# Modulation weights of a two-layer decoder step: from a split pair of products to unsplit float32 in four column strips, in their own buffers

## The chip, the cores and the metric

The kernel runs on one core of a Trainium2 chip. The metric is the device time of one execution in microseconds. Three runs of the kernel before gave 3008.25, 3013.66 and 3019.26 us; their median, 3013.66 us, is the time before.

## What is computed

One inference step of a two-layer decoder for 512 prompt tokens and 8 sample tokens with a model width of 1024. Every sub-layer (feed-forward, mixing, feed-forward) is normalized and then shifted, scaled and gated by vectors that come from a condition `c` (one row for the prompt, eight for the samples, so nine rows):

```
mod = jax.nn.silu(c) @ mod_w + mod_b            # [9 rows] x [1024, 9216], per layer
sh0, sc0, gt0, sh1, sc1, gt1, sh2, sc2, gt2 = jnp.split(mod[:, None, :], 9, axis=-1)
h = modulate(rmsnorm(x, norm_pre[0]), sh0, sc0)
x = x + 0.5 * gt0 * rmsnorm(swiglu(h, ffn1_in, ffn1_out), norm_post[0])
... mixing with sh1, sc1, gt1 ...
h = modulate(rmsnorm(x, norm_pre[2]), sh2, sc2)
x = x + 0.5 * gt2 * rmsnorm(swiglu(h, ffn2_in, ffn2_out), norm_post[2])
```

`swiglu(h, w_in, w_out)` is `(silu(g) * u) @ w_out` with `g, u` the halves of `h @ w_in`; the hidden width is 2816, that is 22 tiles of 128.

## The kernel before

All large products keep float32 accuracy by splitting. A block of weights (a **chunk**: 128 partitions by 1024 float32, 512 KB) is loaded by SP into one of four slots of `stage`. ACT rounds it into `w_hi` (`split`, L856), DVE writes the remainder `lo_apart` (L1970), and TensorE multiplies high with high, high with low and low with high parts of the activations. The four slots form one ring for all weights of the program: `load` (L686) issues a chunk as soon as the chunk four before it has been split (`lo_done`), and ACT and DVE take the chunks in the same order.

A **trip** of the feed-forward input loop (`ffn_in`) makes two hidden tiles. On TensorE (L1442) these are four tiles of 48 matmuls of 260 columns: gate and up of the first hidden tile, gate and up of the second. ACT applies silu to the gate tile (`sil`, L949), DVE multiplies it with the up tile (`hidf`, L2127), ACT and DVE write its high and low part. The weights of a trip are four chunks, c0 to c3.

The modulation weights are 18 **groups** of 512 columns per layer, 36 in all, each group being 4 chunks, so 144 chunks. They go through the same ring. In the opening of layer 0, MOD_FIRST = 8 groups (32 chunks of 1024 columns) are computed before anything else. The other 28 groups run one per trip beside the feed-forward loops (`per` = 8: the four chunks of the trip alternate with four modulation chunks), in phases f1j0, f1i1, f2j0 and f2i1 of layer 0 (five trips each) and f1j0 and f1i1 of layer 1 (five and three). A modulation chunk is four matmuls of 512 columns with the silu of `c` as the stationary operand `c_st` (high and low part, 18 of 128 columns in use), done by `mod_rows` (L1313) after each of the four tiles of a trip. When the group is complete ACT copies its 18 rows (`modrow`, L960), TensorE turns them (`turn_rows`, L1322), and DVE adds the bias into `modT`.

The order within a trip is written by hand on every engine and locked by counting semaphores. What matters here:

- TensorE: the fourth tile of a trip (up of the second hidden tile) is written to the same PSUM pair 0 as the first tile of the next trip, which therefore waits for `hidf` of the second hidden tile (`pe.wait_ge(ev_d, i * 2 + ed)` in `body`, L1460).
- ACT (L941), for each of the two hidden tiles m: two splits, silu, two more splits, the high part `hid_hi`. DVE (L2113) follows with its remainders and `hidf`.
- `mod_rows` of the last chunk stands after the fourth tile, and the rows are turned after the first tile of the next trip.

```
for m in range(2):
    at = per // 2 * m
    if m or split_here(phase, i):
        split(chunk(phase, at + 2, i, per))
    split(chunk(phase, at + 3, i, per))
    ...
    nc.scalar.activation(sil[:, m, :]..., PS[:, 2 * m, :, 0:HALF], ACT.Silu)
```

## Time and profile before

| | |
|---|---|
| runs (us) | 3008.25, 3013.66, 3019.26 |
| span of the profiled execution | 3023.3 us |
| TensorE busy | 96% of the span |
| VectorE / ScalarE / GpSimd busy | 56% / 39% / 12% |
| mean DMA | 107 GB/s |

The profiled execution has no separate time beside its span; the span lies 9.6 us (0.3%) above the median of the three runs. In the profile, PE is the matmul side of TensorE, PEld its weight loads, DVE is VectorE, ACT is ScalarE, POOL is GpSimd, SP is the engine that issues the weight loads. A float32 matmul shows as two records, a matmul of rounded (fp32r) operands as one. The page's rows on the 40 slices show PE at nine tenths or more from slice 2 to 39 and the DMA queues at a quarter to a half of their capacity except in the first slice.

### The profile page before, as it was taken

The numbers are of one execution on the slowest core, as the hardware profiler recorded it, in microseconds if no ns is written. First come the engines' busy times: TensorE is split into PE (matmuls) and PEld (weight loads), VectorE is DVE, ScalarE is ACT, GpSimd is POOL, SyncE is SP. The second block draws the span as 40 slices with busy tenths as digits, with TensorE's granted clock in tenths as the row PEclk, the third lists the DMA queues.
The fourth block names the chain that finished last, engine by engine and source line by source line (L and its number), as shares of the span: only waits on it lengthen the run. The fifth ranks groups of instructions, "written<-read, shape, count | busy, mean of one in ns | idle before, by whom it ended". The sixth has DMA issues, their size and how long they took to land.

```text
span 3023.3 us, 55792 instructions
## 1 busy us (share of the span) xinstructions
PE 2908.2 (96%) x22056; PEld 2703.3 (89%) x22056; DVE 1687.8 (56%) x3427; ACT 1193.3 (39%) x2023; POOL 366.7 (12%) x426
## 2 busy tenths in 40 slices
PE   6999999999999999999999999999999999999998
PEld 5899999899776689999999999999987767999997
DVE  5443346888869475424474424378878775632234
ACT  6533333545444244323334323245453532522222
POOL 2100000324025100000010000011330431100000
PEclk8999999999999999999999999999999999999998
DMA  7443443412224334434434434232222243232321
GB/s 265 127 153 98 141 147 91 137 50 64 57 75 124 107 98 124 145 101 153 124 93 133 141 100 149 86 109 99 57 64 62 62 133 119 85 97 82 100 76 64
DMA packets 448405, 324.28 MB, mean 107 GB/s; under 512 B 25114, under 2 KB 403346, under 8 KB 447451
## 3 DMA queue, kind: packets, MB, share of 16 engines
q1 hardware_dynamic: 442810, 296.60, 32.6%
q0 software_dynamic: 5408, 25.17, 2.5%
q8 instruction: 121, 1.98, 0.3%
q14 instruction: 66, 0.53, 0.1%
HBM read 310.48 MB, written 11.24 MB: 106 GB/s over the span
## 4 chain that ended last, share of the span: by engine, by line
PE 77%; DVE 15%; issue 3%; ACT 2%; DMA 1%; POOL 0%; another core or an unknown queue 0%; ACTq 0%; SPq 0%; DVEq 0%; POOLq 0%
PE PS L1306 77%; DVE score L2514 1%; DVE lo_over L1975 1%; DVE best L2513 1%; DMA stage<-in_mod_w 1%; DVE W L2444 1%; PE PS L1538 1%; DVE score L2504 1%; DVE xT L2071 1%; DMA stage<-in_w_branch_attn 1%; DVE counting L2251 0%; DVE sm L2197 0%; DVE tmpn L2069 0%; DVE lg L2680 0%; DVE dgr L2690 0%
## 5 line engine op out<-in xcount | busy, mean ns | idle before, releaser
L1306 PE MATMUL PS<-h_hi,w_hi 128*128 128x260 f32 (+1 forms) x4000 | 830.4, 289 | 10.5 <-POOL h_lo L2897 5.8
L1306 PE MATMUL PS<-h_lo,w_hi 128*128 128x260 f32 (+1 forms) x4000 | 808.0, 284 | 0.0
L1975 DVE TENSOR_TENSOR lo_apart<-stage,w_hi 128x1024 fp32r<-128x1024 f32 (+2 forms) x448 | 492.9, 1134 | 466.4 <-ACT w_hi L863 462.5
L1306 PEld LDWEIGHTS PS<-h_hi,w_hi 128*128 128x128 f32 (+1 forms) x4000 | 623.4, 189 | 60.5 <-issue 40.3
L1306 PEld LDWEIGHTS PS<-h_lo,w_hi 128*128 128x128 f32 (+1 forms) x4000 | 618.9, 189 | 0.0
L1306 PE MATMUL PS<-h_hi,lo_apart 128*128 128x260 f32 x2816 | 567.2, 283 | 0.0
L863 ACT ACTIVATE w_hi<-stage 128x1024 fp32r<-128x1024 f32 (+3 forms) x586 | 540.9, 954 | 46.8 <-DMA stage<-in_mod_w 15.3
L1306 PEld LDWEIGHTS PS<-h_hi,lo_apart 128*128 128x128 f32 x2816 | 434.6, 189 | 0.0
L1306 PE MATMUL PS<-hid_lo,w_hi 128*128 128x260 f32 x1408 | 283.8, 283 | 0.0
L1306 PE MATMUL PS<-hid_hi,w_hi 128*128 128x260 f32 x1408 | 283.2, 282 | 0.0
L1306 PE MATMUL PS<-hid_hi,lo_apart 128*128 128x260 f32 x1408 | 282.9, 282 | 0.0
L2127 DVE TENSOR_TENSOR hidf<-sil,PS 128x520 f32<-128x520 f32 x88 | 61.3, 697 | 366.5 <-PE PS L1306 366.5
L1306 PE MATMUL PS<-h_hi,lo_over 128*128 128x260 f32 (+1 forms) x1184 | 241.1, 286 | 0.0
L955 ACT ACTIVATE hid_hi<-hidf 128x520 fp32r<-128x520 f32 (+1 forms) x88 | 56.3, 639 | 450.9 <-DVE hidf L2127 450.9
L2878 POOL TENSOR_TENSOR hs<-yT,r_s 128x64 f32<-128x64 f32 x6 | 1.9, 320 | 1853.5 <-ACT r_s L929 1853.5
L1306 PEld LDWEIGHTS PS<-hid_hi,lo_apart 128*128 128x128 f32 x1408 | 217.0, 188 | 0.0
L1306 PEld LDWEIGHTS PS<-hid_hi,w_hi 128*128 128x128 f32 x1408 | 216.8, 188 | 0.1
L1306 PEld LDWEIGHTS PS<-hid_lo,w_hi 128*128 128x128 f32 x1408 | 216.7, 188 | 0.0
L1306 PEld LDWEIGHTS PS<-h_hi,lo_over 128*128 128x128 f32 (+1 forms) x1184 | 184.8, 190 | 0.0
L1975 DVE TENSOR_TENSOR lo_over<-stage,w_hi 128x1024 fp32r<-128x1024 f32 (+1 forms) x138 | 147.2, 1069 | 23.6 <-ACT w_hi L863 22.0
L949 ACT ACTIVATE sil<-PS 128x520 f32<-128x520 f32 x88 | 53.2, 604 | 263.2 <-PE PS L1306 263.2
L1306 PE MATMUL PS<-w_hi,c_st 128*128 128x512 f32 x288 | 116.5, 424 | 11.8 <-DVE lo_apart L1975 11.4
(436 smaller groups left out, 4088.6 us busy)
## 6 DMA issues: line engine op xcount, KB each, us to landing
stage<-in_ffn_in SPq DMA_DIRECT2D x176, 512.0 KB
stage<-in_mod_w SPq DMA_DIRECT2D x144, 512.0 KB
stage<-in_w_in SPq DMA_DIRECT2D x72, 512.0 KB
stage<-in_ffn_out SPq DMA_DIRECT2D x64, 384.0 KB
stage<-in_ffn_out SPq DMA_DIRECT2D x64, 320.0 KB
stage<-in_w_out SPq DMA_DIRECT2D x16, 512.0 KB
x_hold<-xT SPq DMA_DIRECT2D x2, 2080.0 KB
xT<-x_hold SPq DMA_DIRECT2D x2, 2080.0 KB, 8.1
```

What stands on the lines that cost most here:

```text
L863: nc.scalar.activation(w_hi[:, ch.slot, 0:ch.elems], stage[:, ch.slot, 0:ch.elems], ACT.Copy)\
L949: nc.scalar.activation(sil[:, m, :].rearrange("p (a n) -> p a n", a=2), PS[:, 2 * m, :, 0:HALF], ACT.Silu).then_inc(ev_a, 1)
L955: nc.scalar.activation(hid_hi[:, bass.ds(i * 2 + (s.first_tile + m), 1), :], hidf[:, m:m + 1, :], ACT.Copy)\
L1306: return nc.tensor.matmul(out, lhsT, rhs, start=start, stop=stop)
L1538: return nc.tensor.transpose(out, in_, ident[p0:p0 + size, p0:p0 + size])
L1975: nc.vector.tensor_tensor(lows(ch)[:, ch.slot, 0:ch.elems], stage[:, ch.slot, 0:ch.elems], w_hi[:, ch.slot, 0:ch.elems].bitcast(FP32), ALU ...
L2071: nc.vector.tensor_tensor(xT[:, k, 0:T], xT[:, k, 0:T], tmpn[:, k % 2, 0:T], ALU.add).then_inc(x_ready, 1)
L2127: nc.vector.tensor_tensor(hidf[:, m, :].rearrange("p (a n) -> p a n", a=2), sil[:, m, :].rearrange("p (a n) -> p a n", a=2), PS[:, up, :, ...
L2444: own(nc.vector.tensor_tensor_scan(W4[:, r, q, 1:NCH + 1], V(6)[:, g:g + 1].to_broadcast([P, NCH]), W4[:, r, q, 1:NCH + 1], 0.0, ALU.mult, ...
L2504: i = nc.vector.scalar_tensor_tensor(sc, rl[:, n % 2, 0:(t + 1) * P], wT[:, t, h:h + 1], sc, ALU.mult, ALU.add)
L2513: own.step(nc.vector.max(best[:], sc))
L2514: own.step(nc.vector.match_replace(sc, best[:], sc, TAKEN))
```

## The change

1. The modulation products are no longer split. The weights stay float32 and are multiplied in float32 with `c32` (the nine rows of silu(c), padded to 32 columns). Four matmuls of 256 columns go to four strips of 32 PSUM partitions: in the opening the four quarters of a chunk's 1024 columns, beside the feed-forward two k-blocks by two halves of 512 columns, the k-blocks being summed when the rows are turned (`halves_sel`).
2. The modulation chunks leave the ring. In the opening they use eight slots of `mod_open`; beside the loops they use four slots of their own, `mod_stage`, with the semaphores `mod_full` and `mod_used`. The feed-forward chunks keep the ring, now with nothing between them.
3. Four groups in the opening (16 chunks), fourteen beside the first feed-forward of layer 0: two per trip in f1j0 (`rate` = 2, ten groups), one per trip in four trips of f1i1, none in its fifth (`f1j1`).
4. All four chunks of a group are multiplied together, after the tile that ends a hidden tile (both with two groups per trip, the second with one), instead of one chunk after each tile. ACT and DVE in a trip: two splits, silu, `hidf`, `hid_hi`, and nothing in between.

```
 class Chunk:
-    def __init__(self, base, shift, elems, in_place=False):
+    def __init__(self, base, shift, elems, before, in_place=False):
...
-    MOD_FIRST = GROUPS - (FT // 2 - 1)
+    MOD_FIRST = 4
...
         if l == 0:
-            ffn1 = ([Gates('f1i0', 1, 0), Gates('f1j0', n0 - 1, 2, MOD_FIRST, 0, 0, 'after plain')],
-                    [Gates('f1i1', n1, 0, MOD_FIRST + n0 - 1, 0, n0 - 1)])
+            early = 2 * (n0 - 1)
+            left = FIRST_BESIDE - early
+            ffn1 = ([Gates('f1i0', 1, 0), Gates('f1j0', n0 - 1, 2, MOD_FIRST, 0, 0, 'after plain', rate=2)],
+                    [Gates('f1i1', left, 0, MOD_FIRST + early, 0, early),
+                     Gates('f1j1', n1 - left, 2 * left, opening='after mods')])
...
 SP, the opening
-                    for g in range(MOD_PAIRS):
-                        for k in range(4 if g == 0 else 0, KD):
-                            load(chunk('mod', k, g, 8), mod_weights(g, k).unsqueeze(1))
+                    for n in range(4, KD * MOD_PAIRS):
+                        if n >= OPEN:
+                            sp.wait_ge(mod_used, n - OPEN + 1)
+                        sp.dma_start(mod_open[:, n % OPEN, :], mod_weights(n // KD, n % KD)).then_inc(open_full[n % OPEN], 16)
+
+                def mod_load(s, i, m, j):
+
+                    sp.wait_ge(mod_used, i * (4 * s.rate) + (OPENED + 4 * (s.mods_before + m) + j - 3))
+                    sp.dma_start(mod_stage[j][:].rearrange("p (k n) -> p k n", k=2),
+                                 rows_of('mod_w', 2 * j, 2, i * (512 * s.rate) + (s.group + m) * 512, 512, bass.ds(s.of_layer, 1)))\
+                        .then_inc(mod_full[j], 16)
...
 SP, a trip
                         for j in range(4):
-                            load(chunk(phase, j * per // 4, i, per),
+                            load(chunk(phase, j, i, 4),
                                  rows_of(name, 0, KD, (j % 2) * DFF + (f0 + s.first_tile + i * 2 + j // 2) * P, P))
-                            if per == 8:
-                                load(chunk(phase, 2 * j + 1, i, per),
-                                     rows_of('mod_w', 2 * j, 2, i * 512 + s.group * 512, 512, bass.ds(s.of_layer, 1)))
+                            if s.group is not None:
+                                if type(i) is int and i == j == 0 and phase in ('f1j0', 'f2j0'):
+                                    sp.wait_ge(h_lo_ready, (N + (1 if phase == 'f1j0' else 3)) * KD)
+                                if s.rate == 1:
+                                    mod_load(s, i, 0, j)
+                                else:
+                                    mod_load(s, i, j // 2, 2 * (j % 2))
+                                    mod_load(s, i, j // 2, 2 * (j % 2) + 1)
...
 ACT, a trip
                         for m in range(2):
-                            at = per // 2 * m
                             if m or split_here(phase, i):
-                                split(chunk(phase, at + 2, i, per))
-                            split(chunk(phase, at + 3, i, per))
+                                split(chunk(phase, 2 * m + 2, i, 4))
+                            split(chunk(phase, 2 * m + 3, i, 4))
...
                             nc.scalar.activation(sil[:, m, :].rearrange("p (a n) -> p a n", a=2),
                                                  PS[:, 2 * m, :, 0:HALF], ACT.Silu).then_inc(ev_a, 1)
-                            if per == 8:
-                                split(chunk(phase, at + 4, i, per))
-                                split(chunk(phase, at + 5, i, per))
...
 TensorE, products and turning
-                def mod_rows(pair, ch, j):
-
-                    pe.wait_ge(lo_done, ch.number(1))
-                    for k in range(2):
-                        for w in (w_hi, lows(ch)):
-                            last = mm(PS[:, pair, 0, :], c_st[:, 2 * j + k, :], w[:, ch.slot, k * 512:(k + 1) * 512],
-                                      start=(j == 0 and k == 0 and w is w_hi), stop=(j == 3 and k == 1 and w is not w_hi))
-                    last.then_inc(chunk_used, 1)
+                def mod_rows(s, i, m, j):
+
+                    pe.wait_ge(mod_full[j], i * (16 * s.rate) + 16 * (OPENED // OPEN + s.mods_before + m + 1))
+                    for q in range(4):
+                        odd, half = q // 2, q % 2
+                        last = mm(PS[32 * q:32 * q + 32, 3, 0, 0:256], c32[:, 2 * j + odd, :],
+                                  mod_stage[j][:, odd * 512 + half * 256:odd * 512 + half * 256 + 256],
+                                  start=(j == 0), stop=(j == 3))
+                    last.then_inc(mod_used, 1)
 
                 def turn_rows(pair):
-                    for q in range(4):
-                        last = mm(PS[:, pair, 1, q * NC:(q + 1) * NC], modrow[:, q * P:(q + 1) * P], sel18[:])
+                    by_block = PS[:, pair, 1, 0:4 * NC].rearrange("p (h q c) -> p q h c", h=2, q=2)
+                    for q in range(2):
+                        last = mm(by_block[:, q], modrow[:, q * P:(q + 1) * P], halves_sel[:].rearrange("p (h c) -> p h c", c=NC))
...
 TensorE, a trip
-                                if per == 8:
-                                    mod_rows(3, chunk(phase, 4 * m + 2 * gu + 1, i, per), 2 * m + gu)
+                                if gu == 0 and beside and (m and s.rate == 2 or not m and not (type(i) is int and i == 0)):
+                                    turn_beside(i, m)
+                                if gu == 1 and beside and (m or s.rate == 2):
+                                    for j in range(4):
+                                        mod_rows(s, i, m if s.rate == 2 else 0, j)
```

How the instructions move, at the three places of which the prediction speaks. First the queue of SP, in the loop of phase f1i1 of layer 0 (one group per trip). Before:

```order
L693 ISA [waits lo_done]
L693 DMA stage<-in_ffn_in 128x8x128
L691 REGISTER_ALU
L693 ISA [waits lo_done]
L693 DMA stage<-in_mod_w 128x2x512
L691 REGISTER_ALU
L693 ISA [waits lo_done]
L693 DMA stage<-in_ffn_in 128x8x128
```

And now:

```order
L717 ISA [waits lo_done]
L717 DMA stage<-in_ffn_in 128x8x128
L729 REGISTER_ALU
L730 ISA [waits mod_used]
L730 DMA mod_stage_84<-in_mod_w 128x2x512
L713 REGISTER_ALU
L717 ISA [waits lo_done]
L717 DMA stage<-in_ffn_in 128x8x128
```

The second feed-forward chunk of a trip (c1) stands in both behind the first modulation load; that load now waits for `mod_used`, which TensorE raises, where it waited for `lo_done`, which DVE raises.

Second, ACT in the second half (m = 1) of a trip of the same loop. Before, where the slots 2 and 3 hold c3 and the last modulation chunk of the trip itself:

```order
L862 REGISTER_ALU [waits stage_full2]
L863 ACTIVATE w_hi<-stage 128x1024 [waits chunk_used]
L862 REGISTER_ALU [waits stage_full3]
L863 ACTIVATE w_hi<-stage 128x1024 [waits chunk_used]
L947 REGISTER_ALU
L948 REGISTER_ALU [waits chunk_used]
L949 ACTIVATE sil<-PS 128x520 [waits ev_d]
```

And now, where the slots 0 and 1 hold c0 and c1 of the next trip:

```order
L902 ACTIVATE w_hi<-stage 128x1024 [waits chunk_used,stage_full0]
L899 REGISTER_ALU [waits stage_full1]
L902 ACTIVATE w_hi<-stage 128x1024 [waits chunk_used]
L983 REGISTER_ALU
L984 REGISTER_ALU [waits chunk_used]
L985 ACTIVATE sil<-PS 128x520 [waits ev_d]
```

The silu that closes a trip now stands behind the split of c1 of the next trip; before it stood behind chunks of its own trip only.

Third, TensorE at the end of a hidden tile in f1j0, now:

```order
L1340 MATMUL PS<-mod_stage_84,c 32x256 [waits mod_full0]
L1340 MATMUL PS<-mod_stage_84,c 32x256 x3
L1340 MATMUL PS<-mod_stage_85,c 32x256 [waits mod_full1]
L1340 MATMUL PS<-mod_stage_85,c 32x256 x3
L1340 MATMUL PS<-mod_stage_86,c 32x256 [waits mod_full2]
L1340 MATMUL PS<-mod_stage_86,c 32x256 x3
L1340 MATMUL PS<-mod_stage_87,c 32x256 [waits mod_full3]
L1340 MATMUL PS<-mod_stage_87,c 32x256 x3
L1340 MATMUL PS<-h_hi,w_hi 128x260 [waits lo_done,ev_a]
```

All sixteen products of a group stand together; before, four stood after each tile.

## Rows read from the trace of the kernel before

**Rows 1.** The page: span, and busy time of each engine with its share.
```profile
span 3023.3 us, 55792 instructions
PE 2908.2 (96%) x22056; PEld 2703.3 (89%) x22056; DVE 1687.8 (56%) x3427; ACT 1193.3 (39%) x2023; POOL 366.7 (12%) x426
```

**Rows 2.** The page: the chain that ended last, shares by engine.
```profile
PE 77%; DVE 15%; issue 3%; ACT 2%; DMA 1%; POOL 0%; another core or an unknown queue 0%; ACTq 0%; SPq 0%; DVEq 0%; POOLq 0%
```

**Rows 3.** Windows: length, engines' busy time, clock, DMA share, GB/s (opening, trip, ffn_out).
```profile
40.00:60.00 20.00, 17.91 (x71) 13.28 (x71) 15.16 (x14) 14.02 (x15) 3.68 (x3) 0.83 0.88 296
151.40:179.50 28.10, 28.10 (x218) 26.96 (x218) 12.44 (x13) 10.66 (x14) 0.00 (x0) 1.00 0.49 150
280.00:300.00 20.00, 20.00 (x169) 20.00 (x168) 3.66 (x4) 4.14 (x6) 0.00 (x0) 1.00 0.31 90
```

**Rows 4.** Timeline of SP: start, length, two trips apart; then a pair of loads.
```profile
151.34 0.38 SPq L693 DMA_DIRECT2D stage<-in_ffn_in  x1
...
179.43 0.38 SPq L693 DMA_DIRECT2D stage<-in_ffn_in  x1
...
131.72 0.37 SPq L693 DMA_DIRECT2D stage<-in_ffn_in  x1
132.88 0.37 SPq L693 DMA_DIRECT2D stage<-in_mod_w  x1
```

**Rows 5.** Timeline of PE: rows turned, then one modulation chunk, then the tile.
```profile
148.13 1.05 PE L1306 MATMUL PS<-sel,modrow 18*128 18x9 f32 x8
149.12 0.50 PE L1306 MATMUL PS<-w_hi,c_st 128*128 128x512 f32 x1
...
155.90 0.39 PE L1306 MATMUL PS<-w_hi,c_st 128*128 128x512 f32 x1
...
156.83 0.40 PE L1306 MATMUL PS<-h_hi,w_hi 128*128 128x260 f32 x2
```

**Rows 6.** Timeline of PE in the mixing stage: float32 products in four 32-column strips.
```profile
656.60 0.40 PE L1306 MATMUL PS<-h_hi,lo_over 128*128 128x260 f32 x2
656.93 0.67 PE L1306 MATMUL PS<-CA,BXl 128*32 128x128 f32 x16
657.53 0.51 PE L1306 MATMUL PS<-h_hi,w_hi 128*128 128x260 f32 x2
```

**Rows 7.** Groups of instructions: busy us, mean ns of one, idle before.
```profile
L863 ACT ACTIVATE w_hi<-stage 128x1024 fp32r<-128x1024 f32 (+3 forms) x586 | 540.9, 954 | 46.8 <-DMA stage<-in_mod_w 15.3 <-PE PS L1306 11.4 <-DMA stage<-in_w_in 9.2
L1975 DVE TENSOR_TENSOR lo_apart<-stage,w_hi 128x1024 fp32r<-128x1024 f32 (+2 forms) x448 | 492.9, 1134 | 466.4 <-ACT w_hi L863 462.5
L2127 DVE TENSOR_TENSOR hidf<-sil,PS 128x520 f32<-128x520 f32 x88 | 61.3, 697 | 366.5 <-PE PS L1306 366.5
L955 ACT ACTIVATE hid_hi<-hidf 128x520 fp32r<-128x520 f32 (+1 forms) x88 | 56.3, 639 | 450.9 <-DVE hidf L2127 450.9
```

**Rows 8.** Timeline: loads issued with the queues idle, and splits as they land.
```profile
20.89 3.73 SPq L693 DMA_DIRECT2D stage<-in_mod_w  x4
...
24.44 1.06 ACT L863 ACTIVATE w_hi<-stage 128x1024 fp32r<-128x1024 f32 x1 [1.46 <-DMA stage<-in_mod_w]
...
28.12 1.06 ACT L863 ACTIVATE w_hi<-stage 128x1024 fp32r<-128x1024 f32 x1
29.40 1.06 ACT L863 ACTIVATE w_hi<-stage 128x1024 fp32r<-128x1024 f32 x1 [0.22 <-DMA stage<-in_mod_w]
```

**Rows 9.** Windows of one us after the pair of loads at 131.72 and 132.88.
```profile
133.00:134.00 1.00, 1.00 (x11) 1.00 (x10) 0.00 (x0) 0.00 (x0) 0.00 (x0) 1.00 0.82 231
134.00:135.00 1.00, 1.00 (x9) 0.91 (x8) 0.00 (x0) 0.34 (x1) 0.00 (x0) 1.00 1.17 338
135.00:136.00 1.00, 1.00 (x9) 0.92 (x8) 0.00 (x0) 1.00 (x2) 0.00 (x0) 1.00 0.96 335
136.00:137.00 1.00, 1.00 (x11) 1.00 (x10) 0.69 (x1) 1.00 (x2) 0.00 (x0) 1.00 0.32 121
```

**Rows 10.** Windows: a stretch without matmuls, and the stretch after it.
```profile
17.30:20.90 3.60, 0.00 (x0) 0.00 (x0) 2.13 (x7) 2.35 (x3) 0.00 (x0) 1.00 0.00 0
20.90:24.30 3.40, 3.38 (x8) 2.71 (x9) 3.37 (x3) 2.08 (x3) 1.26 (x1) 0.50 0.68 206
```

**Rows 11.** Timeline of ACT at the end of the opening.
```profile
72.57 1.06 ACT L863 ACTIVATE w_hi<-stage 128x1024 fp32r<-128x1024 f32 x1 [0.59 <-DMA stage<-in_mod_w]
...
80.00 1.28 ACT L919 ACT_TABLE_LOAD   x1
82.98 0.27 ACT L919 ACTIVATE std<-PS,eps 128x5 f32<-128x5 f32 x1 [1.69 <-PE PS L1306]
```

More of the change, by code:

```diff
@@ L127, in mods_added @@
     def mods_added(l):
-        return 1 + FT // 2 - 1 + l * GROUPS
+        return 1 + FIRST_BESIDE + l * GROUPS
     OUT_PAIRS = (1, 0, 2, 3)
     def in_phases(segments):
-        return [(s.phase, 4 * s.trips * (s.per // 4), BLK, 2 * s.trips, 2 * s.trips) for s in segments]
+        return [(s.phase, 4 * s.trips, BLK, 2 * s.trips, 2 * s.trips) for s in segments]
     plans = []
@@ L450, in build @@
     vec_in = sem("vec_in")
+    mod_full = [sem(f"mod_full{q}") for q in range(MOD_SLOTS)]
+    mod_used = sem("mod_used")
+    open_full = stage_full + mod_full
     def mod_weights(g, k):
@@ L515, in _ @@
             pool.memset(r_s[:], 1.0).then_inc(consts_ready, 1)
+            own.wait()
+            steps_taken['pool'] = own.n
         @block.scalar
@@ L936, in ffn_in @@
                 def ffn_in(s):
-                    phase, per = s.phase, s.per
+                    phase = s.phase
                     ea, ed = evicts_a[phase], evicts_d[phase]
@@ L956, in body @@
                                 .then_inc(hid_hi_ready, 1)
-                        if per == 8:
-                            act.wait_ge(chunk_used, chunk(phase, 7, i, per).number(1))
-                            act.wait_ge(rows_turned, i + (MOD_PAIRS + s.mods_before))
-                            nc.scalar.activation(modrow[:], PS[0:2 * NC, 3, 0, :], ACT.Copy).then_inc(rows_copied, 1)
+                            if s.group is not None and (m == 1 or s.rate == 2):
+                                n = m if s.rate == 2 else 0
+                                act.wait_ge(mod_used, i * (4 * s.rate) + (OPENED + 4 * (s.mods_before + n) + 4))
+                                act.wait_ge(rows_turned, i * s.rate + (MOD_PAIRS + s.mods_before + n))
+                                nc.scalar.activation(modrow[:], PS[:, 3, 0, 0:256], ACT.Copy).then_inc(rows_copied, 1)
                         if type(i) is int and i == 0 and phase == 'f2j0':
@@ L1339, in mod_pair @@
                     for k in range(KD):
-                        ch = chunk('mod', k, g, 8)
-                        pe.wait_ge(lo_done, ch.number(1))
+                        n = KD * g + k
+                        pe.wait_ge(open_full[n % OPEN], 16 * (n // OPEN + 1))
                         if k == 0 and g >= 2:
                             pe.wait_ge(ev_a, g - 1)
-                        for w in (w_hi, lows(ch)):
-                            for half in range(2):
-                                last = mm(PS[:, 2 * (g % 2), half, :], c_st[:, k, :], w[:, ch.slot, half * 512:(half + 1) * 512],
-                                          start=(k == 0 and w is w_hi), stop=(k == KD - 1 and w is not w_hi))
-                        last.then_inc(chunk_used, 1)
+                        for q in range(4):
+                            last = mm(PS[32 * q:32 * q + 32, 2 * (g % 2), 0, 0:256], c32[:, k, :],
+                                      mod_open[:, n % OPEN, q * 256:(q + 1) * 256], start=(k == 0), stop=(k == KD - 1))
+                        last.then_inc(mod_used, 1)
                         if k == 2 and g == 0:
@@ L1442, in ffn_in @@
                 def ffn_in(s, j=None):
-                    phase, per = s.phase, s.per
+                    phase, beside = s.phase, s.group is not None
                     ea, ed = evicts_a[phase], evicts_d[phase]
@@ L1480, in body @@
                                         pe.wait_ge(mod_added, mods_added(l))
-                                tile(pair, [(chunk(phase, (2 * m + gu) * per // 4, i, per), 0, KD, P)], (h_hi, h_lo),
+                                tile(pair, [(chunk(phase, 2 * m + gu, i, 4), 0, KD, P)], (h_hi, h_lo),
                                      h_waits=h_waits if m == gu == 0 else None)
@@ L1497, in ffn_in @@
                     each(pe, s.trips, trip, last=False)
-                    if per == 8:
+                    if beside:
                         turn_beside(s.trips)
@@ L2134, in body @@
                                                     ALU.subtract).then_inc(hid_lo_ready, 1)
+                            if first_group is not None and s.rate == 2 and (m or not (type(i) is int and i == 0)):
+                                rows_beside(i, m)
                     each(dve, s.trips, body)
-                    if per == 8:
+                    if first_group is not None:
                         rows_beside(s.trips)
```

192 lines of the change are left out of this document (98 added, 94 removed).

## The prediction

> **What bounds the kernel now.** I read the page first. TensorE is busy for 2908 of 3023.3 us [rows 1], and the chain that ended last runs over it for 77% and over VectorE, in the mixing stage for the most part, for 15% [rows 2]. So an edit pays where it takes work from TensorE, and costs where it makes TensorE wait. Then the windows, by stage [rows 3]: in the opening TensorE waits for weights (296 GB/s, the clock at 0.83); in a trip with modulation beside the feed-forward it never waits (28.10 busy of 28.10 us, DMA at 0.49 of its capacity), and VectorE and ScalarE are under half busy. What the change takes from those two is worth nothing there. A trip lasts 28.1 us, from 151.34 to 179.43 [rows 4]. A pure matmul stretch does 169 in 20 us, 118 ns each [rows 3], so a tile of 48 is 5.7 us.
>
> **Gain 1, products beside the loops.** A modulation chunk before: from 155.90 to 156.83, 0.93 us; turning a group's rows: 148.13 to 149.12, 0.99 us [rows 5]. A group is 4 x 0.93 + 0.99 = 4.7 us, 28 groups are 132 us, all on TensorE. For the new form the nearest row is in the mixing stage: 16 float32 records of 128 columns in four strips take 0.60 us with the changes of form on either side [rows 6], against 16 x 0.11 = 1.8 us one after another. The strips do run side by side. Of the 0.60 about 0.16 is the change to strips and back (the step from 656.60 to 656.93 has 0.33 where two plain records take 0.24, and it ends with a like gap), which leaves 0.44: 0.11 for each round of four. A chunk is now 8 records of 256 columns, two rounds of twice 0.107 us: 0.43 us. A group: 4 x 0.43 + 0.16 + half of 0.99 for turning (4 records for 8) = 2.4 us; 32 groups are 76 us. **Minus 56 us.** The Trainium skill (TensorE: Matmul & The Clock Gate, Part 3: Packing small matmuls) gives measured speedups of 3.07 for four row strips and 2.38 for three column strips, not 4 and 3; by that a chunk would be some 0.56 us, and the sum, as an estimate, some 17 us worse. The trace disagrees: four records fit where one does. The bound on the other side is no overlap at all, 8 x 0.21 = 1.7 us per chunk (a rival).
>
> **Gain 2, the opening.** 16 chunks fewer. Before, the last modulation chunk was split at 72.57 and the root of the norm was done at 83.25 [rows 11]. Now twelve chunks are still to be loaded at about 18.4 us (the first four land earlier), into eight slots and without splits, so the loads run at the queues' pace. With idle queues the first lands 3.55 us after its issue at 20.89, later ones 1.28 us apart [rows 8]: 18.4 + 3.55 + 11 x 1.28 = 36. Then c0 to c2 of the first trip at 1.5 us each: 40.8, the split 1, the table load 1.28, the root 0.27: 43.4. That is 40 us earlier; at the opening's pace of 296 GB/s [rows 3], 1.77 us a chunk, it is 34. The squares, eight at under 2 us, are through by then. I take **minus 38 us**. Sixteen chunks move under the loops; f1j0 then needs 12 chunks a trip, 6.3 MB, which at 335 GB/s [rows 9] is 19 us of at least 28.
>
> **Loss 1, the wait that the change adds.** It is not in the products but in SP's queue. A modulation load now waits until TensorE has used the chunk that lay in its slot, and there are four slots for a group of four. All products of a group stand at the end of the trip. So SP stops behind the first modulation load from shortly after c0 of the next trip is issued until the end of the trip, and c1 of the next trip is queued behind it. ACT has to split that c1 before it does the silu that closes the trip, DVE makes its remainder before `hidf`, and the first tile of the next trip waits for that `hidf`. Before, all of it had been loaded ahead, and the silu stood behind chunks of its own trip. Counted from E, when the first chunk's four products are done and the slot is free:
> - The modulation load goes first, c1 second. One load alone lands 3.55 us after its issue [rows 8]; a second adds 524 KB at 335 GB/s, 1.56 us [rows 9]. The pair at 131.72 and 132.88 [rows 4] was through between 136 and 137 [rows 9], which agrees. With the wake-up: E + 5.2.
> - Split 0.95, remainder 1.13, `hidf` 0.70 [rows 7], hops 0.2: E + 8.2.
> - TensorE has the other three chunks to do meanwhile, 3 x 0.43: it is free at E + 1.3, and **waits 6.9 us**.
>
> This happens between any two trips of a phase with one group per trip: 3 times in f1i1 (four trips), 4 in f2j0, 4 in f2i1, and in layer 1 4 in f1j0 and 2 in f1i1 (three trips): 17 x 6.9 = 117 us. The last trip of a phase is free of it, since the next phase's loads stand behind nothing that waits. With two groups per trip (f1j0 of layer 0) two modulation loads, the second a product later, stand ahead of c1: E + 6.9, so the wait is 8.6 us; 4 x 8.6 = 34. In the middle of such a trip c3 is held in the same way, but TensorE has the third tile to do: there it waits at the turning of the rows, behind split, remainder, `hidf`, `hid_hi` 0.64 [rows 7] and the copy of the rows (taken as 0.5): 6.9 + 4.2 = 11.1 against 1.3 + 5.7 = 7.0: 4.1 us, five times: 20. Together **plus 171 us**.
>
> **Loss 2, the clock.** A stretch of 3.6 us without matmuls was followed by 3.4 us at 0.50 of the clock, 1.2 GHz [rows 10]: 1.7 us lost. Each of the 21 long waits has such a stretch and more, so at least that: **plus 36 us**; below, nothing (the drop may fall inside the wait), above, twice as much. Fewer splits, the new selector and the moved gate vectors lie beside TensorE's work and are taken as nothing; were TensorE to wait for ACT elsewhere, it would show as a new row of waits.
>
> A rule that speaks against the strips stands in the Trainium skill (TensorEngine Tiling (Array Packing), Key Properties): changing the tiling mode drains the engine. The trace agrees that a change costs something, 0.16 us for a pair of them [rows 6], and it is in the sum. It gives no number of its own; if the whole 0.60 were the cost of a pair, the sum would be 14 us worse.
>
> **The sum.** 3023.3 - 56 - 38 + 171 + 36 = 3136 us of span. The profiled execution lies 0.3% above the median of the runs, so for the median 3136 x 3013.66 / 3023.3 = **3126 us**, 3.7% slower.
>
> **The rivals.**
> - *The waits come as worked out but the clock costs nothing* (the drop ends within the wait): 3100 span, 3090. Against it: 20.90 to 24.30 [rows 10] is all work at the lower level. Chance 0.16; it lies in the range.
> - *Faster: the waits stay within their cover.* Place: c1 of the next trip. It decides at 94 us of gains over 26 waits, 3.6 us each. For that c1 would have to be in `stage` within some 1.9 us of its issue. A single load took 3.55 [rows 8], and nothing in the trace is faster; it needs an error in my reading of the queue, so that SP gets past the modulation load earlier. With no waits at all: 3023 - 94 = 2929, for the median 2920. Chance 0.07, and 0.02 for landing within 0.3%.
> - *The burst slows c1 down.* Eight loads are now issued at once, where two were in flight before. If they share the queues rather than follow each other, c1 lands with the middle of 4.2 MB, some 4 us later: 21 x 4 = 84 more, 3220 span, 3210. Against it: in the pair the first was not held up by the second. Chance 0.07.
> - *The change doesn't do what it says: the strips run one after another.* A chunk is 1.7 us, a group 7.3 with turning, 32 of them 235 us against 132, plus 103. But the longer products cover part of the waits (free at E + 5.1): 17 x 3.1 + 4 x 6 + 5 x 1 = 82, clock 10, opening -33: 3185, for the median 3175. Against it stands [rows 6]. Chance 0.06.
>
> **How the numbers follow.** The forecast as worked out has 0.62, the rivals what stands with them. A measurement of this kernel can tell about 0.3%, 9 us, from no change. Faster: 0.07; within 0.3%: 0.02; slower: the rest, 0.91. For the range: low, no clock loss, loads 1 us sooner in 26 waits, gains of 66 and 42: 3023 + 171 - 26 - 108 = 3060 span, 3050. High: loads 1.5 us later (39), twice the clock loss and some for the short waits (80), gains of 50 and 33: 3023 + 171 + 39 + 80 - 83 = 3230, 3220. The slowed burst's and the serial strips' times fall inside; left out are the faster case and extremes of the others.
>
> **What would show it right or wrong.** Right: in the loops with modulation PE has idle time before its first tile of a trip, released by DVE `hidf`, and ACT's split sat idle for `stage<-in_ffn_in` before it; SP's longest waits are for PE at the modulation load; trips of about 34 us where they were 28.1, and some 43 in f1j0; the clock below 1.00 in the loops; 32-column products with 8 records in 0.43 us; the first tiles at about 52 us instead of 92. Wrong: trips of about 26 us with PE busy throughout (the faster case: then SP isn't held); products of a group taking near 7 us (serial strips); c1 landing well after 5.2 us (slowed burst).

## The result, and the profile after

| | before | after |
|---|---|---|
| median of the runs, us | 3016.32 (4 runs, 3008.25 to 3019.26) | 3175.41 (4 runs, 3163.75 to 3182.08) |
| ratio, 95% interval | | 1.0531 [1.0502, 1.0561] |
| profiled execution: span, us | 3023.3 | 3162.0 |
| mean granted clock | 0.974 | 0.948 |

The change makes the kernel 5.3% slower. The forecast was 3126 us with a range of 3050 to 3220: right in sign and in mechanism, and 49 us too low. The profiled execution after is the fastest of its four, so spans differ by 139 us where medians differ by 159.

The page after, span and busy time of the engines; what answers to it before is [rows 1].

```profile
span 3162.0 us, 56102 instructions
PE 2854.8 (90%) x22476; PEld 2651.1 (84%) x22476; DVE 1517.2 (48%) x3284; ACT 1049.5 (33%) x1881; POOL 361.5 (11%) x427
```

DVE lost 171 us of work and ACT 144, and nothing was gained by it. TensorE is busy for 53 us less than before, although part of its work now runs at half clock, and the span is 139 us longer: the time went into TensorE's waiting.

Groups of instructions on the page after: busy us and mean ns of one, then the idle time ahead of them and its releaser.

```profile
L1340 PE MATMUL PS<-h_hi,w_hi 128*128 128x260 f32 (+1 forms) x4000 | 853.9, 296 | 178.2 <-DVE hidf L2154 168.0
L902 ACT ACTIVATE w_hi<-stage 128x1024 fp32r<-128x1024 f32 (+4 forms) x442 | 398.1, 924 | 488.9 <-DMA stage<-in_ffn_in 464.3
```

The waits after, by engine, line and releaser: us in total, times, longest.

```profile
PE PS L1340 <- DVE hidf L2154: 168.0, 21, 9.5
PE PS L1340 <- DVE modT L2140: 23.0, 5, 6.6
PE PS L1340 <- ACT modrow L994: 4.0, 1, 4.0
SPq L730 <- PE PS L1340: 632.5, 27, 28.8
```

21 waits ahead of a trip's first tile, 168.0 us, and 5 in the middle of f1j0's trips, 26.5 us: one of 4.0 for `modrow` in the first trip, then four of 4.6 to 6.6 for `modT`. (The fifth wait for `modT` is 0.57 us at the end of the phase.) Together 194.5 us, and just the number and the places of the prediction. ACT in its turn waits for the feed-forward's weights, and SP stands at the modulation load (line 730) for up to 28.8 us. One of the waits, in f2j0, in the order of time (SP, ACT, DVE and PE rows; start, length, and in brackets the idle time before):

```profile
1235.04 1.93 PE L1340 MATMUL PS<-mod_stage,c 128*32 128x256 f32 x32
1235.90 0.41 SPq L730 DMA_DIRECT2D mod_stage<-in_mod_w  x1
1236.56 0.37 SPq L717 DMA_DIRECT2D stage<-in_ffn_in  x1
...
1241.59 1.06 ACT L902 ACTIVATE w_hi<-stage 128x1024 fp32r<-128x1024 f32 x1 [15.58 <-DMA stage<-in_ffn_in]
1242.55 0.59 ACT L985 ACTIVATE sil<-PS 128x520 f32<-128x520 f32 x1
1242.68 1.23 DVE L2011 TENSOR_TENSOR lo_apart<-stage,w_hi 128x1024 fp32r<-128x1024 f32 x1 [15.41 <-ACT w_hi L902]
1243.82 0.69 DVE L2154 TENSOR_TENSOR hidf<-sil,PS 128x520 f32<-128x520 f32 x1
...
1244.64 0.80 PE L1340 MATMUL PS<-h_hi,w_hi 128*128 128x260 f32 x2 [7.41 <-DVE hidf L2154]
...
1269.70 1.93 PE L1340 MATMUL PS<-mod_stage,c 128*32 128x256 f32 x32
```

The group's products start at 1235.04. Once the first of its four chunks is through, SP gets past the modulation load (1235.90), and only then issues c1 of the next trip (1236.56). c1 is split 5.0 us after that (the splits of before follow their load's issue by 3.55 us with the queues idle [rows 8]), and silu, remainder, `hidf` and the tile follow it one by one. ACT had been idle for 15.58 us: nothing but the late load held the silu back. The next group follows 34.7 us later; a trip took 28.1 before [rows 4].

What comes behind such a wait, in windows (span of time: length, busy time of PE, PEld, DVE, ACT, POOL with their instructions; granted clock, DMA share, GB/s):

```profile
1269.00:1271.00 2.00, 2.00 (x31) 1.35 (x33) 0.00 (x0) 0.00 (x0) 0.00 (x0) 1.00 0.00 0
1271.70:1279.10 7.40, 0.00 (x0) 0.00 (x0) 1.93 (x3) 1.55 (x2) 0.00 (x0) 0.72 1.04 316
1279.30:1281.30 2.00, 2.00 (x9) 2.00 (x10) 0.87 (x2) 1.79 (x3) 0.00 (x0) 0.50 1.11 322
1281.30:1283.30 2.00, 2.00 (x11) 2.00 (x10) 1.05 (x1) 0.55 (x1) 0.00 (x0) 0.50 1.08 349
1283.30:1285.30 2.00, 2.00 (x11) 2.00 (x11) 1.23 (x1) 0.52 (x1) 0.00 (x0) 0.52 0.80 207
1285.30:1287.30 2.00, 2.00 (x19) 2.00 (x19) 0.00 (x0) 0.00 (x0) 0.00 (x0) 1.00 0.00 0
```

The clock falls inside the wait and stays at its lower level for six us of work behind it: 9 to 11 records in 2 us where 19 fit. This one cost 3 us. Note the first window too: DMA share 0.00 in the last 2 us of a trip. The queues are idle there, with room in the ring, because SP isn't allowed past.

The opening after (PE, ACT, PE). The root of the norm is at 45.82 where it was at 82.98 [rows 11], 37.2 us earlier, and the first tile starts at 54.99.

```profile
23.77 0.64 PE L1340 MATMUL PS<-mod_open,c 128*32 128x256 f32 x8 [0.65 <-DMA mod_open<-in_mod_w]
25.06 0.64 PE L1340 MATMUL PS<-mod_open,c 128*32 128x256 f32 x8 [0.65 <-DMA mod_open<-in_mod_w]
...
45.82 0.27 ACT L956 ACTIVATE std<-PS,eps 128x5 f32<-128x5 f32 x1
...
54.99 0.64 PE L1340 MATMUL PS<-h_hi,w_hi 128*128 128x260 f32 x2
```

### The profile page after: what moved, and what is told of

It reads as the page before. It is cut to its first block, busy times and chain, and to the rows that moved or that the text cites. A ratio compares the mean times of both kernels' runs of the same rounds, so it can differ in the third digit from the quotient of the medians.

```text
span 3162.0 us, 56102 instructions
## 1 busy us (share of the span) xinstructions
PE 2854.8 (90%) x22476; PEld 2651.1 (84%) x22476; DVE 1517.2 (48%) x3284; ACT 1049.5 (33%) x1881; POOL 361.5 (11%) x427
## 4 chain that ended last, share of the span: by engine, by line
PE 69%; DVE 16%; DMA 6%; issue 4%; ACT 3%; SPq 1%; POOL 0%; DVEq 0%; another core or an unknown queue 0%; ACTq 0%; POOLq 0%
PE PS L1340 69%; DMA stage<-in_ffn_in 5%; DVE score L2545 1%; DVE lo_over L2011 1%; DVE best L2544 1%; ACT w_hi L902 1%; DVE W L2475 1%; DMA stage<-in_w_branch_attn 1%; PE PS L1574 1%; DVE score L2535 1%; DVE hidf L2154 1%; DVE counting L2282 1%; DVE xT L2102 1%; DVE cand L2228 0%; DVE lg L2711 0%
## 5 line engine op out<-in xcount | busy, mean ns | idle before, releaser
L1340 PE MATMUL PS<-h_hi,w_hi 128*128 128x260 f32 (+1 forms) x4000 | 853.9, 296 | 178.2 <-DVE hidf L2154 168.0
L1340 PEld LDWEIGHTS PS<-h_hi,w_hi 128*128 128x128 f32 (+1 forms) x4000 | 638.2, 195 | 224.7 <-DVE lo_apart L2011 177.7
L1340 PE MATMUL PS<-h_lo,w_hi 128*128 128x260 f32 (+1 forms) x4000 | 824.2, 288 | 0.0
L2011 DVE TENSOR_TENSOR lo_apart<-stage,w_hi 128x1024 fp32r<-128x1024 f32 (+2 forms) x304 | 321.5, 1085 | 707.8 <-ACT w_hi L902 704.6
L1340 PEld LDWEIGHTS PS<-h_lo,w_hi 128*128 128x128 f32 (+1 forms) x4000 | 636.8, 194 | 0.0
L1340 PE MATMUL PS<-h_hi,lo_apart 128*128 128x260 f32 x2816 | 585.2, 290 | 0.0
L902 ACT ACTIVATE w_hi<-stage 128x1024 fp32r<-128x1024 f32 (+4 forms) x442 | 398.1, 924 | 488.9 <-DMA stage<-in_ffn_in 464.3
L1340 PEld LDWEIGHTS PS<-h_hi,lo_apart 128*128 128x128 f32 x2816 | 453.3, 197 | 0.0
L2160 DVE TENSOR_TENSOR hid_lo<-hidf,hid_hi 128x520 fp32r<-128x520 f32 (+1 forms) x88 | 61.6, 701 | 74.9 <-ACT hid_hi L988 74.9
```

Source lines behind the costliest of these rows:

```text
L902: nc.scalar.activation(w_hi[:, ch.slot, 0:ch.elems], stage[:, ch.slot, 0:ch.elems], ACT.Copy)\
L1340: return nc.tensor.matmul(out, lhsT, rhs, start=start, stop=stop)
L2011: nc.vector.tensor_tensor(lows(ch)[:, ch.slot, 0:ch.elems], stage[:, ch.slot, 0:ch.elems], w_hi[:, ch.slot, 0:ch.elems].bitcast(FP32), ALU ...
L2160: nc.vector.tensor_tensor(hid_lo[:, f, :], hidf[:, m:m + 1, :], hid_hi[:, f, :].bitcast(FP32), ALU.subtract).then_inc(hid_lo_ready, 1)
```

## The experiments

The theory: the loss is SP's order. The modulation load waits for the end of the group's products and stands ahead of c1 (and in f1j0 of c3), so each such place costs a wait and some clock behind it; the products and the opening do gain what was worked out. Rivals: the strips or the change to strips cost more than their row said; the clock falls for another reason than the waits; the gains aren't there. The first four runs were timed beside the kernel before at 3012.88 us (14 runs), the next two at 3018.87, the last at 3019.5.

**1. Both c blocks ahead of the modulation loads.** SP's order in a trip, of the changed kernel:

```
...
+                        elif s.rate == 1:
+                            block(0)
+                            block(1)
+                            early()
+                            for j in range(2):
+                                mod_load(s, i, 0, j)
+                                block(2 + j)
+                            mod_load(s, i, 0, 2)
+                            mod_load(s, i, 0, 3)
+                        else:
+                            for m in range(2):
+                                block(2 * m)
+                                block(2 * m + 1)
+                                if m == 0:
+                                    early()
+                                for j in range(4):
+                                    mod_load(s, i, m, j)
```

`block(j)` is the load of c_j, `early()` the wait for `h_lo_ready` that was there before.

> Edit of the changed kernel: SP issues the two feed-forward chunks that the closing silu and the next tile need (c0 and c1 of a trip; with two groups per trip also c2 and c3) before the modulation loads that wait for TensorE. Nothing else moves. Theory (the waits come from c1 being queued behind a load that waits for mod_used): the 26 waits go, 21 long ones of 7.4 to 9.5 us and 5 short ones of 4.0 to 6.6, 194 us in all, with some 61 us of lower clock after them; the span falls from 3162 to about 2907 to 2929, a time of about 2925 us, 0.97 of before. Rival 1 (eight loads in a burst saturate the queues): the burst is still there, the waits shrink by a part, time 3050 to 3150. Rival 2 (the strips or the change of tiling mode cost the time): nothing changes, 3175 us.

Measured: **2920.76 us** (4 runs, 2915.33 to 2925.77), ratio to before 0.9683 [0.9653, 0.9713]. The page of this run:

```profile
span 2913.6 us, 56102 instructions
PE 2804.6 (96%) x22476; PEld 2603.4 (89%) x22476; DVE 1518.4 (52%) x3284; ACT 1052.6 (36%) x1881; POOL 361.4 (12%) x427
L1357 PE MATMUL PS<-h_hi,w_hi 128*128 128x260 f32 (+1 forms) x4000 | 832.6, 289 | 9.9 <-DVE lo_over L2028 6.0
```

The same instructions, the same number of them, 255 us less. The waits for `hidf` are gone (178.2 us of idle time before this group have become 9.9). A line of SP's order decides between 5.3% slower and 3.2% faster. This is the version that beats both kernels. PE in this run, three trips:

```profile
1146.01 1.93 PE L1357 MATMUL PS<-mod_stage,c 128*32 128x256 f32 x32
...
1171.58 1.93 PE L1357 MATMUL PS<-mod_stage,c 128*32 128x256 f32 x32
...
1197.16 1.93 PE L1357 MATMUL PS<-mod_stage,c 128*32 128x256 f32 x32
```

A trip with one group is 25.6 us, 2.5 less than the 28.1 of before [rows 4]. 22 trips are of that kind (32 groups less the ten of f1j0): 55 us, and 37 from the opening make 92, the difference to before (3012.88 - 2920.76). Measured over the three loops with modulation, each from its first to its last `hidf`, it is 57.5 us (1058.5 before, 1001.0 here); the trips of f1j0 take with two groups what they took with one.

**2. The same, only in phases with one group per trip.** f1j0 of layer 0 keeps the order of the change:

```
...
+                        else:
+                            for j in range(4):
+                                block(j)
+                                if j == 0:
+                                    early()
+                                mod_load(s, i, j // 2, 2 * (j % 2))
+                                mod_load(s, i, j // 2, 2 * (j % 2) + 1)
```

> The same edit in the phases with one group per trip only; f1j0 of layer 0, with two groups per trip, keeps the changed kernel's order. Theory: 17 waits of 7.7 us and 36 us of clock go, the 4 of 9.3 and 5 of 5.3 us in f1j0 with 24 us of clock stay: about 88 us above e1_order, some 3010 us, no better than the kernel before. Rival (the waits feed each other across phases): e2 and e1 differ by much more or much less than 88 us.

Measured: **3010.91 us** (10 runs, 2995.26 to 3015.82), ratio 0.9979 [0.9960, 0.9998]. The waits of this run:

```profile
PE PS L1356 <- DVE hidf L2170: 37.2, 4, 9.6
PE PS L1356 <- DVE modT L2156: 20.8, 5, 5.2
```

So 17 waits are worth 3175.4 - 3010.9 = 164.5 us, 9.7 each, and the nine places in five trips of f1j0 are worth 3010.9 - 2920.8 = 90 us: some 61 of waiting (37.2, 20.2 of the 20.8, and 4.0 for `modrow`) and 22 of work at half clock behind the waits, by the trace; the other 7 lie within what executions differ by. f1j0 alone would have eaten all that the change gains: this kernel runs within 0.2% of the one before.

**3. One modulation chunk after each tile again,** as before the change, in phases with one group per trip; SP's order as changed:

```
-                                if gu == 1 and beside and (m or s.rate == 2):
+                                if beside and s.rate == 1:
+                                    mod_rows(s, i, 0, 2 * m + gu)
+                                elif gu == 1 and beside:
```

> SP's order is left as changed; instead TensorE multiplies one modulation chunk after each of the four tiles of a trip, as before the change, in the phases with one group per trip. Theory: the first slot is free a tile into the trip, SP passes the modulation load three tiles earlier, c1 lands in time and the 17 waits go as in e2_order_single, for three more changes of tiling mode per trip at 0.16 us, 22 x 3 x 0.16 = 11 us: about 3020 us. Rival (it is SP's order by itself, whenever the slot comes free): the waits stay, 3175 us. Rival (changing the tiling mode is dear, 0.6 us each): about 3050 us.

Measured: **3039.46 us** (5 runs, 3029.43 to 3042.27), ratio 1.0063 [1.0038, 1.0089]. SP's order is the same as in the change, and the 17 long waits are gone: it takes both, the queue's order and all products at the trip's end. But it is 28.6 us slower than experiment 2, between the two values expected. PE of this run:

```profile
1299.54 0.64 PE L1340 MATMUL PS<-mod_stage,c 128*32 128x256 f32 x8
1300.54 0.51 PE L1340 MATMUL PS<-h_hi,w_hi 128*128 128x260 f32 x2 [0.37 <-DVE hidf L2156]
...
1313.05 0.41 PE L1340 MATMUL PS<-h_hi,lo_apart 128*128 128x260 f32 x2
1313.40 0.64 PE L1340 MATMUL PS<-mod_stage,c 128*32 128x256 f32 x8
1313.96 0.51 PE L1340 MATMUL PS<-h_hi,w_hi 128*128 128x260 f32 x2
1314.31 0.40 PE L1340 MATMUL PS<-h_lo,w_hi 128*128 128x260 f32 x2
```

Two plain groups of records start 0.24 us apart. From 1313.05 to 1314.31 are 1.26 us; less two such steps and the chunk's 0.43, one change to the strips and back costs **0.35 us**, in the steps on both sides of it. Three more of them in each of 22 trips are 23 us, and the short wait of 0.37 us, 16 times, 6: 29 for the 28.6 measured.

**4. A fill of the wait that comes too late.** 30 products of 512 columns ahead of TensorE's wait for `hidf` (`ev_d`), but behind a wait for `mod_added`, in all phases but f2j0, that is at 17 of the 21 long waits:

```
+                                        if phase != 'f2j0':
+                                            pe.wait_ge(mod_added, i * s.rate + s.mods_before)
+                                            kept_running(PS[:, 3, 1, :], 30)
```

> The changed kernel, with 30 idle products of 512 columns (about 6.4 us) put into 17 of the 21 long waits (not in f2j0) before TensorE waits for hidf. They compute nothing that is used. Theory (the clock's drop costs work after the wait): the clock stays up, the 17 waits are as long as before, and 17 x 2.2 = 37 us are saved: about 3138 us. Rival (the drop falls within the wait and costs nothing): 3175 us.

Measured: **3251.32 us** (4 runs, 3247.7 to 3257.96), ratio 1.0768 [1.0739, 1.0798]: slower, not faster. The edit missed its aim. The fill waits for `mod_added`, which DVE raises when it has added up the modulation vectors, and the trace has that addition after the split of the same late c1. So 13 of the 17 fills started only when the long wait was over. The waits of this run show it:

```profile
PE PS L1340 <- DVE modT L2143: 135.2, 18, 12.7
```

Those 13 waits are 6.9 to 12.7 us long; the other five of this row are the ones of f1j0. Four fills, each in the second trip of a phase with one group per trip, started at once. 13 fills of 6.4 us on top, less 2 us each for the four, are 75 us; measured are 76. Neither theory of the expectation had this case.

**5. The same fill in fewer places,** only in the phases with one group per trip but f2j0 (13 waits). The edit puts it just where experiment 4 had it, so the expectation's "unlike the fill before" is wrong:

```
+                                        if s.rate == 1 and phase != 'f2j0':
+                                            pe.wait_ge(mod_added, i * s.rate + s.mods_before)
+                                            kept_running(PS[:, 3, 1, :], 30)
                                         pe.wait_ge(ev_d, i * 2 + ed)
```

> The changed kernel with 30 products of 512 columns (about 6.4 us) put ahead of TensorE's wait for hidf, at the start of every second and later trip of a phase with one group per trip, other than f2j0: 13 of the 21 long waits. Unlike the fill before, TensorE waits for nothing ahead of these products but its own earlier trip, so they lie inside the wait of 7.7 us and 1.3 us of it stay. They write a bank that nothing reads at that time; the results are unchanged. Theory A (the stretch without matmuls costs clock behind it, 2.1 us for each of these waits): 13 x 2.1 = 27 us come back, 3175 - 27 = 3148, and the granted clock in the trips of f1i1, f2i1 and of the first feed-forward of layer 1 stays at 1.00. Theory B (the clock falls for another reason, such as the 32-column products, and the waits cost only their own length): 3175, no change, with the half-speed stretches still there behind 13 trips. Theory C (the fill again isn't inside the wait): 3175 + 13 x 6.4 = 3258.

Measured: **3216.55 us** (4 runs, 3215.05 to 3218.29), ratio 1.0662 [1.0642, 1.0682]. Between A and C, and the trace shows why. Four fills started at once and nine didn't. One of each (PE):

```profile
401.20 7.10 PE L1340 MATMUL PS<-c_st 128*128 128x512 f32 x30
408.80 0.50 PE L1340 MATMUL PS<-h_hi,w_hi 128*128 128x260 f32 x2 [0.50 <-DVE hidf L2157]
...
441.55 3.78 PE L1340 MATMUL PS<-c_st 128*128 128x512 f32 x8 [7.11 <-DVE modT L2143]
```

My expectation had named only the bank, and not the wait for `mod_added` that the edit itself contains. Where the fill started at once (401.20), the tile behind it starts at full speed. Nine fills of 6.4 us on top, less 2 us each for the other four, are 50 us; measured are 41.

**6. Products twice.** Experiment 1 with each modulation chunk beside the feed-forward multiplied twice (q from 0 to 3 two times over), so that these modulation vectors come out doubled:

```
-                    for q in range(4):
+                    for twice in range(8):
+                        q = twice % 4
...
```

> The kernel with c0 and c1 ahead of the modulation loads (2921 us), and every modulation chunk beside the feed-forward multiplied twice into the same sums, so that the modulation vectors of those groups come out doubled. 28 groups of four chunks: 112 chunks more. Theory A (four strips run side by side, a chunk is 0.43 us of TensorE, and TensorE is what ends each trip): 112 x 0.43 = 48 us more, 2969 us. Rival (the strips run one after another, 1.7 us a chunk): 190 us more, 3111 us. Rival (the products lie in slack of the trip and cost nothing): 2921 us.

Measured: **2977.08 us** (4 runs, 2974.33 to 2977.7), ratio 0.9864 [0.9845, 0.9882]; 56.3 us over experiment 1. My count of chunks was wrong, the price right: there are 32 groups beside the loops (1024 records of 32), 128 chunks, and 128 x 0.43 = 55. The group's products in the trace:

```profile
1254.75 3.66 PE L1357 MATMUL PS<-mod_stage,c 128*32 128x256 f32 x64
```

(3.66 - 1.93) / 4 = 0.43 us a chunk, to the hundredth the 0.43 of the prediction. The strips run side by side in full, and every bit of TensorE's work in these trips shows in the time.

**7. The fill at last inside the wait.** The 30 products go into the bank of the trip's second tile, which was emptied in the middle of the trip before, in all 21 places:

```
                                     if not (type(i) is int and i == 0):
+                                        pe.wait_ge(ev_d, i * 2 + (ed - 1))
+                                        kept_running(PS[:, 1, 0, :], 30)
                                         pe.wait_ge(ev_d, i * 2 + ed)
```

> The changed kernel with the same 30 products of 512 columns ahead of the wait for hidf, at the start of every second and later trip of all phases with modulation (all 21 long waits), and now into the PSUM bank of the trip's second tile, which DVE emptied in the middle of the trip before; so nothing they wait for is held by the late c1. In the run before this one, of 13 fills one started at once (the second trip of f1i1: 30 products in 7.10 us inside the wait, 0.50 us idle left, full clock behind it) and the others waited for the modulation vectors' sum, which DVE makes after the same late split, so that they came on top. The results are unchanged. Theory A (a stretch without matmuls costs clock behind it, 2.1 us for a wait with one group per trip and 2.7 in f1j0 of layer 0): 17 x 2.1 + 4 x 2.7 = 46 us come back, 3175 - 46 = 3129 us; some 0.5 us of each of the 17 waits stays and about 2 us of the four of 9.3. Theory B (the clock falls for another reason): 3175 us, with the half-speed stretches still behind the trips.

(The expectation says that one of experiment 5's 13 fills started at once; the trace has four.)

Measured: **3132.68 us** (4 runs, 3125.52 to 3135.64), ratio 1.0361 [1.0330, 1.0391]. 630 products more, and the kernel is 42.7 us faster than the change; expected were 46. PE of this run, and windows over the same trip (columns as above):

```profile
1238.08 1.93 PE L1340 MATMUL PS<-mod_stage,c 128*32 128x256 f32 x32
1240.03 7.06 PE L1340 MATMUL PS<-c_st 128*128 128x512 f32 x30
1248.05 0.50 PE L1340 MATMUL PS<-h_hi,w_hi 128*128 128x260 f32 x2 [0.96 <-DVE hidf L2156]
```

```profile
1240.00:1247.00 7.00, 7.00 (x33) 5.56 (x31) 0.92 (x1) 1.55 (x2) 0.00 (x0) 1.00 1.03 305
1248.00:1250.00 2.00, 1.95 (x16) 1.96 (x17) 0.70 (x1) 1.97 (x4) 0.00 (x0) 1.00 1.14 321
1250.00:1252.00 2.00, 2.00 (x19) 2.00 (x19) 1.22 (x1) 0.61 (x1) 0.00 (x0) 1.00 1.07 349
```

The tile starts no sooner, `hidf` is as late as ever; but behind it the clock is 1.00 where it was 0.50, 19 records in 2 us where there were 9 to 11. So it is the stretch without matmuls that lets the clock fall, not the products in strips ahead of it, which stayed; and it is worth 2.0 us for each of the 21 long waits, in the mean. In f1j0, where 2.3 to 3.7 us of each wait stay open behind the fill, three of the four are still followed by 1.7 us lost at half clock.

## Why the prediction was right, and where it was off

| step | predicted, us | measured, us | from |
|---|---|---|---|
| products beside the loops | -56 | -57.5 | the three loops, experiment 1 against before |
| opening | -38 | -37.2 | the root at 45.82, before 82.98 |
| waits | +171 | +194.5 | the waits after |
| clock | +36 | +58 | work at half clock in the loops with modulation, see below |
| sum of the four | +113 | +158 | medians: 3175.41 - 3016.32 = 159 |

- **The mechanism was right, and it is shown.** 21 + 5 waits where 21 + 5 were counted; SP stands at the modulation load; moving c1 ahead of it takes all of them away (experiment 1), or the 17 outside f1j0 (experiment 2), and using up the slots one by one takes the same 17 away (experiment 3).
- **Waits: mis-sized, 24 us.** "The pair ... with the wake-up: E + 5.2": the 17 waits between trips with one group took 7.4 to 8.3 us, 7.7 in the mean, where 6.9 was worked out. At 1235.04 the products begin, the first chunk is through 0.5 us later, SP's load stands at 1235.90 and c1's at 1236.56, and the split starts at 1241.59: some 6 us after the slot is free. The chain behind it, split to tile, took 3.05 us (1241.59 to 1244.64) where 2.98 stood in the prediction. So it is the load, and a few tenths the wake-up (1235.90 is 0.4 us after the first chunk, where E + 5.2 left 0.1): I took two loads issued 1.16 us apart with one just landed [rows 8, 9], and here c1 is the second of eight loads, and the third is issued 0.6 us behind it. In f1j0 the waits are 9.3 us for 8.6, in the middle of its trips 5.3 in the mean for 4.1. That the burst slows c1 was a rival with 4 us more at each place; what happened is a small part of it, under 1 us. I did not try fewer loads in the burst, so this share is argued and not shown.
- **Clock: mis-sized, 22 us.** "At least 1.7 us for each of the 21": added up from the trace after, the 21 long waits are followed by 46 us lost, 2.2 each, and the fill of experiment 7 gave 42.7 back, 2.0 each. The other 12 us lie behind the five waits in the middle of f1j0's trips, 1.8 to 2.7 each. The sum had these at nothing, without a reason ("some for the short waits" stands only in the upper bound of the range), although at the 4.1 us forecast for each they were longer than the stretch of 3.6 that gave the price [rows 10]. For f1j0 I had forecast trips of some 43 us; they take 48 (below). In experiment 1, without the waits, these loops have no work at half clock.

The work behind two of the five waits in the middle of a trip, all at half clock (columns as above):

```profile
102.20:107.60 5.40, 5.40 (x25) 5.40 (x26) 1.62 (x2) 1.06 (x1) 0.00 (x0) 0.50 0.01 3
150.50:155.40 4.90, 4.90 (x22) 4.90 (x23) 1.23 (x1) 0.69 (x1) 0.00 (x0) 0.50 0.02 3
```

Over the whole program TensorE was busy at half clock for 139 us before and 218 after; half of the 79 more is 40 us, less than 58, because the stretches outside the loops lost 61 us behind the norm's root before and 45 after. That differs between executions (50 to 61 in experiments 1, 2 and 7) and is part of why the span after is so short.

The Trainium skill (TensorE: Matmul & The Clock Gate, What's actually happening) calls the ramp's penalty under 1% of a typical kernel's span; by the fill it is 1.3% here, paid 21 times over.

PE after, the tiles behind two long waits in f1j0, one trip apart:

```profile
122.42 0.80 PE L1340 MATMUL PS<-h_hi,w_hi 128*128 128x260 f32 x2 [9.45 <-DVE hidf L2154]
...
170.36 0.80 PE L1340 MATMUL PS<-h_hi,w_hi 128*128 128x260 f32 x2 [9.31 <-DVE hidf L2154]
```

- **Products: right as a sum, from two terms that are each a little off.** The chunk is 0.43 us, as said. The change to strips and back is 0.35 us and not 0.16: I read it from the step ahead of the strips [rows 6] and took the other side as a like gap, without counting that the first tile records behind it are late as well (0.35 us to the next, 1313.96 to 1314.31, and not 0.24). On the other hand turning the rows costs 0.46 and not 0.5. A group is 4 x 0.43 + 0.35 + 0.46 = 2.5 us instead of 2.4, and a group of before cost 5.0 (28.1 against the 23.1 of a trip without modulation) where 4.7 was added up. The Trainium skill (TensorEngine Tiling (Array Packing), Key Properties) says that changing the tiling mode drains the engine; the trace agrees in so far as a pair of changes costs 0.35 us. With SP's order right, that makes one place per group the better choice: experiment 3 pays for three more a trip. The Trainium skill's speedup of 3.07 for four row strips (TensorE: Matmul & The Clock Gate, Part 3: Packing small matmuls) is not what happens here; four float32 column strips of 256 columns take the time of one (0.43 us, see the last section).
- **Opening: right.** 37.2 of 38.
- The measured terms add up to 3016.3 - 57.5 - 37.2 + 194.5 + 58 = 3174 us, for the median of 3175.4. Of the 49 us that the forecast was low, 24 are the waits' and 22 the clock's, and 3 come from the kernel before (3016.3 with the fourth run, 3013.7 when I forecast).
- **Rivals.** No clock cost: refuted by experiment 7. Waits that stay covered: what experiment 1 gives, 2920.76, at the very time worked out for it (2920), but it took another order on SP. Serial strips had the nearest time of all, 3175, by accident: their products would take 7 us a group, and they take 1.93. A time that fits is no evidence for a cause.

## What to carry to other kernels

A load that waits for a consumer must not stand in a queue ahead of a load that needn't wait and is needed sooner: issue what is due next first, and let the slot's wait stand last. With four slots and all four emptied at the trip's end, the whole queue moves in step with that end, however much room the other ring has. When an edit takes work off engines with slack and the time goes up, look for the idle stretch of DMA just ahead of the wait (share 0.00 at the end of each trip here) and for what the issuing queue stands at. And a wait of TensorE of some 7 us costs about 2 us more than its length, in the clock behind it, and one of 4.0 to 6.6 us here hardly less; if it can't be removed, products into a free bank give that back, provided that nothing they wait for hangs on the same late load.

## What the runs showed of the hardware

- Four float32 products of 256 columns in four strips of 32 output partitions take 0.43 us a set (8 records), in doubled number still 0.43 each. One such product alone has two records of 0.21 each (by the records of 256, 384 and 512 columns of `kT,qT` before, with 64 rows in use, 428, 535 and 641 ns: 0.107 us for 128 columns), so four strips take the time of one.
- One change to the strips and back costs 0.35 us between float32r tiles, part of it in the two steps behind the change.
- The stretch at half clock behind a wait of 7.7 us differs from wait to wait, between 1.4 and 3.1 us of time lost; the mean is what can be planned with. Waits of 4.0 to 6.6 us in f1j0 cost about as much, 1.8 to 2.7 us, and so did three of the four places of experiment 7 where 2.3 to 3.7 us of a wait stayed open behind the fill (1.7).
- The modulation chunks in the opening land 1.29 us apart at first (23.77 and 25.06), as the split ones of before did (1.28) [rows 8]; TensorE waits for each.
